# Latent pages of seven sequences turned in 32x32 blocks on VectorE instead of on TensorE

## The reference

```python
def _mla_keys(kv_lat, k_rope, w_uk, g_k_head):
    k_nope = jnp.einsum('btl,lhd->bthd', kv_lat, w_uk)
    k_r = jnp.broadcast_to(k_rope[:, :, None, :], k_nope.shape[:-1] + (QK_ROPE,)).astype(k_nope.dtype)
    return _rmsnorm(jnp.concatenate([k_nope, k_r], axis=-1), g_k_head)
...
    def absorb(carry, kv_blk, kr_blk, mask):
        m, l, acc = carry
        k = _mla_keys(kv_blk, kr_blk, w_uk, g_k_head).astype(jnp.float32)
        sc = jnp.einsum('bshd,bphd->bhsp', qf, k) * scale
...
        acc = acc * corr[..., None] + jnp.einsum('bhsp,bpl->bhsl', p, kv_blk.astype(jnp.float32))
```

## Time and profile before

| | |
|---|---|
| median of three runs | 1144.9 us (1142.89 to 1145.04) |
| the profiled execution's own time | 1145.37 us |
| its span in the profile | 1143.5 us |
| busy, share of the span | PE 98%, PEld 95%, DVE 68%, ACT 51%, POOL 6% |
| the pages of sequences 0 to 7 | about 389 to 811 us of the span |

### The profile page before, as it was taken

The page is one execution under the profiler, slowest core; times in us unless marked ns, Lnnn a source line. Parts: engine busy times, 40 slices in busy tenths (PEclk is TensorE's granted clock), DMA queues, the critical chain, the costliest instruction groups (busy, mean ns, idle before and its releaser), DMA issues.

```text
span 1143.5 us, 25908 instructions
## 1 busy us (share of the span) xinstructions
PE 1122.7 (98%) x9549; PEld 1086.8 (95%) x9549; DVE 778.4 (68%) x1325; ACT 581.7 (51%) x1153; POOL 67.8 (6%) x136
## 2 busy tenths in 40 slices
PE   5999999999999999999999999999999999999998
PEld 3899999999898899999999999999999999999998
DVE  4655553567777688888888888888757666555543
ACT  3444453346576655455545454554566545444432
POOL 2000000010000100101010110101020010000000
PEclk9999999999999999999999999999999999999999
DMA  9987578947344440021211202032257684555552
GB/s 324 314 292 269 183 254 289 348 167 222 99 142 127 133 133 2 20 65 33 52 47 36 62 22 73 13 84 71 57 150 254 227 272 131 183 183 177 177 184 71
DMA packets 165629, 169.84 MB, mean 149 GB/s; under 512 B 25780, under 2 KB 144071, under 8 KB 165525
## 3 DMA queue, kind: packets, MB, share of 16 engines
q1 hardware_dynamic: 163799, 166.83, 45.6%
q10 hardware_dynamic: 1742, 1.88, 0.5%
HBM read 167.13 MB, written 2.49 MB: 148 GB/s over the span
## 4 chain that ended last, share of the span: by engine, by line
PE 92%; DVE 2%; SPq 2%; ACT 1%; DMA 1%; issue 1%; POOL 0%; DVEq 0%; ACTq 0%
PE PS L1894 27%; PE PS L1895 27%; PE PS L1896 27%; PE PS L1971 2%; SPq L451 2%; PE PS L2367 1%; PE PS L2342 1%; PE PS L2343 1%; DMA raw<-in_w_ffn_in 1%; PE PS L2288 1%; PE PS L2099 1%; PE PS L2308 0%; PE PS L2338 0%; DVE wL L1172 0%; PE PS L2287 0%
## 5 line engine op out<-in xcount | busy, mean ns | idle before, releaser
L1172 DVE TENSOR_TENSOR wL<-raw,wH 128x1024 fp32r<-128x1024 f32 (+2 forms) x208 | 246.3, 1191 | 209.8 <-ACT wH L717 208.4
L717 ACT ACTIVATE wH<-raw 128x1024 fp32r<-128x1024 f32 (+2 forms) x208 | 213.2, 1029 | 245.6 <-PE PS L1896 224.7
L1894 PE MATMUL PS<-uH,wH 128*128 128x264 f32 x1024 | 294.2, 287 | 4.5 <-DVE uL L1233 4.0
L1895 PE MATMUL PS<-uL,wH 128*128 128x264 f32 x1024 | 291.8, 285 | 0.0
L1896 PE MATMUL PS<-uH,wL 128*128 128x264 f32 x1024 | 291.4, 285 | 0.0
L1894 PE MATMUL PS<-wqH,kTH 128*128 128x336 f32 (+2 forms) x768 | 255.7, 333 | 0.0
L1896 PE MATMUL PS<-wqH,kTL 128*128 128x336 f32 (+2 forms) x768 | 246.1, 320 | 0.0
L1895 PE MATMUL PS<-wqL,kTH 128*128 128x336 f32 (+2 forms) x768 | 245.9, 320 | 0.0
L1894 PEld LDWEIGHTS PS<-uH,wH 128*128 128x128 f32 x1024 | 193.9, 189 | 7.9 <-issue 6.4
L1895 PEld LDWEIGHTS PS<-uL,wH 128*128 128x128 f32 x1024 | 194.2, 190 | 0.0
L1896 PEld LDWEIGHTS PS<-uH,wL 128*128 128x128 f32 x1024 | 193.6, 189 | 0.0
(11 more groups left out here) (343 smaller groups left out, 1497.8 us busy)
## 6 DMA issues: line engine op xcount, KB each, us to landing
raw<-in_w_ffn_in SPq DMA_DIRECT2D x86, 512.0 KB, 3.5
adaw<-in_w_ada SPq DMA_DIRECT2D x72, 512.0 KB, 6.5
raw<-in_w_ffn_out SPq DMA_DIRECT2D x32, 512.0 KB, 3.5
raw<-in_w_in SPq DMA_DIRECT2D x32, 512.0 KB, 4.5
kv<-in_cache_kv_latent SPq DMA_DIRECT2D x128, 128.0 KB, 2.0
raw<-in_w_ffn_out SPq DMA_DIRECT2D x16, 384.0 KB, 3.0
raw<-in_w_attn_out SPq DMA_DIRECT2D x8, 512.0 KB, 4.1
raw<-in_w_conv_out SPq DMA_DIRECT2D x8, 512.0 KB, 4.7
```

Source lines behind the costliest of these rows:

```text
L717: f(wH[:, k, 0:width], raw[:, k, 0:width], ACT.Copy).then_inc(w_hi, 1)
L1172: v.tensor_tensor(wL[:, k, 0:width], raw[:, k, 0:width], wH[:, k, 0:width].bitcast(F32), ALU.subtract).then_inc(w_lo, 1)
L1894: mm(dst, a[0], b[0], start=start, stop=False)
L1895: mm(dst, a[0], b[1], start=False, stop=False)
```

## The change

For sequences 1 to 7 TensorE no longer turns the latent pages. SP copies a group of four pages inside SBUF from `kv2` into `kx`, in four transfers; transfer q takes columns 32q to 32q+31 of each half of each page and puts them into partitions 32q to 32q+31, in runs of 32 elements. VectorE transposes `kx` (128x1024) in blocks of 32x32 into `kT32`, once for a group, in steps 2, 6, 10 and 14, ahead of kTL, for the group that begins two pages later. Each has two buffers; together they take the place of `raw`, which is free between the gate weights of sequence 0 and the end of the pages. In `kT32` the tokens of a page stand in four parts; `kTH` is written through a permuted view (neighbours 4 elements apart), and kTL reads and writes in that view too, so the keys' product reads the same layout as before. kTH waits for the counter `kx_ps` instead of `kT_ps`, and for `kr_ps` where it reads rotary keys. Sequence 0 stays with TensorE.

`VALUES_PAGE` goes from 10 to 8 and the taps are given out anew. SP's loop over the sequences is written out, with the copies between the loads; `gate_quad(1)` is asked for after the last kTL.

```diff
-VALUES_PAGE = 10
-TAPS = (0, 1, 1, 0, 2, 2, 1, 2, 2, 2, 7, 3, 2, 3, 1, 2)
+VALUES_PAGE = 8
+TAPS = (0, 0, 0, 0, 2, 2, 1, 2, 5, 2, 2, 4, 3, 4, 2, 2)
...
+        kx = sb("kx", [P, 2, 4 * KL], at=ring)
+        kT32 = sb("kT32", [P, 2, 4 * KL], at=ring + 8192)
...
+        def turned_page(n):
+            return kT32[:, n // 4 % 2, :].rearrange("p (k a h t) -> p a h k t", k=4, a=4, h=2)[:, n % 4, :, :, :]
...
+            def pages_next(b, g):
+
+                sp.wait_ge(pg_rel, 4 * b + g + 1)
+                page_group(b, b % 2, g)
+
+            def blocks(b, g):
+
+                grp = 4 * (b - 1) + g
+                sp.wait_ge(kv2_in[4 * (b % 2) + g], 128 * (b // 2) + 128)
+                if grp >= 2:
+                    sp.wait_ge(kx_ps, grp - 1)
+                pages = kv2[:, NPG * (b % 2) + 4 * g:NPG * (b % 2) + 4 * g + 4, :].rearrange(
+                    "p a (h q i) -> p (a h) q i", q=4, i=QUAD)
+                for q in range(4):
+                    sp.dma_start(kx[QUAD * q:QUAD * q + QUAD, grp % 2, :], pages[:, :, q, :]).then_inc(kx_in[grp % 2], 16)
+
+            def sequence_loads(b):
+
+                if b >= 1:
+                    blocks(b, 2)
+                    blocks(b, 3)
+                if 1 <= b < NB - 1:
+                    pages_next(b + 1, 0)
+                if b < NB - 1:
+                    blocks(b + 1, 0)
+                if 1 <= b < NB - 1:
+                    pages_next(b + 1, 1)
+                    pages_next(b + 1, 2)
+                if b < NB - 1:
+                    blocks(b + 1, 1)
+                if 1 <= b < NB - 1:
+                    pages_next(b + 1, 3)
...
-            with sp.Fori(1, 4) as i:
-                sample_pages(i, 0)
-                sample_pages(i, 1)
+            sp.wait_ge(w_lo, 4 * Q_GATE + 4)
+            for b in range(NB):
+                sequence_loads(b)
+            sp.wait_ge(kTL_done, PAGES + 2)
             with sp.Fori(1, 4) as i:
                 gate_quad(i)
...
+            def page_hi(b, n, turned=False):
+                pg = NPG * b + n
+                if turned:
+                    act.wait_ge(kT_ps, n + 1)
+                else:
+                    act.wait_ge(kx_ps, 4 * b + n // 4 - 3)
                 act.wait_ge(kn_ps, pg + 1)
                 if n % 4 == 0:
+                    act.wait_ge(kr_ps, 8 * b + n // 2 + 1)
                     f(krT[:, (n // 4) % 2, :], PS[:, 0, KL:KL + P], ACT.Copy)
-                f(kTH[:, n % 2, :], PS[:, 0, 0:KL], ACT.Copy).then_inc(kTH_done, 1)
+                if turned:
+                    f(kTH[:, n % 2, :], PS[:, 0, 0:KL], ACT.Copy).then_inc(kTH_done, 1)
+                else:
+                    f(kTH[:, n % 2, :].rearrange("p (h t k) -> p h k t", h=2, k=4), turned_page(n), ACT.Copy
+                      ).then_inc(kTH_done, 1)
...
+            def turn_group(b, g):
+
+                dve.wait_ge(kx_in[g % 2], 128 * b + 64 * (g // 2) - 64)
+                dve.wait_ge(kTL_done, NPG * b + 4 * g - 2)
+                v.transpose(kT32[:, g % 2, :], kx[:, g % 2, :]).then_inc(kx_ps, 1)
+
+            def page_lo(pg, n, b, s, first, turned=False):
 
 
                 dve.wait_ge(kTH_done, pg + 1)
                 if n % 4 == 1:
+                    dve.wait_ge(kr_ps, 8 * b + n // 2 + 2)
                     own.wait()
                     own.done(v.tensor_copy(Srope[:, s, n - 1:n + 3, :],
                                            PS[:, 0, 384:448].rearrange("p (j h) -> p j h", h=H)))
                 if n == 10 and not first:
                     denominators(b - 1)
-                v.tensor_tensor(kTL[:, n % 2, :], PS[:, 0, 0:KL], kTH[:, n % 2, :].bitcast(F32), ALU.subtract
-                                ).then_inc(kTL_done, 1)
+                lo_, hi_ = kTL[:, n % 2, :], kTH[:, n % 2, :].bitcast(F32)
+                if turned:
+                    v.tensor_tensor(lo_, PS[:, 0, 0:KL], hi_, ALU.subtract).then_inc(kTL_done, 1)
+                else:
+                    v.tensor_tensor(lo_.rearrange("p (h t k) -> p h k t", h=2, k=4), turned_page(n),
+                                    hi_.rearrange("p (h t k) -> p h k t", h=2, k=4), ALU.subtract
+                                    ).then_inc(kTL_done, 1)
...
+                    if n % 4 == 2:
+                        if n + 2 < NPG:
+                            if not first:
+                                turn_group(b, (n + 2) // 4)
+                        elif not last:
+                            turn_group(b + 1, 0)
                     if not (last and n == NPG - 1):
-                        page_lo(pg + 1, (n + 1) % NPG, b, s, first)
+                        page_lo(pg + 1, (n + 1) % NPG, b, s, first, first and n + 1 < NPG)
...
-            def turn(use, s, n, pg, b, first):
+            def turn(use, s, n, pg, b, first, turned=False):
...
-                tr(PS[:, 0, 0:128], kv2[:, NPG * s + n, 0:128], ident)
-                tr(PS[:, 0, 128:256], kv2[:, NPG * s + n, 128:256], ident).then_inc(kT_ps, 1)
+                if turned:
+                    tr(PS[:, 0, 0:128], kv2[:, NPG * s + n, 0:128], ident)
+                    tr(PS[:, 0, 128:256], kv2[:, NPG * s + n, 128:256], ident).then_inc(kT_ps, 1)
```

More of the change, by code:

```diff
@@ L169, in decoder_layer @@
         vecT = sb("vecT", [P, V_N])
+        gains = base[0]
         gbc = sb("gbc", [P, B_N])
@@ L356, in decoder_layer @@
         kv2_in = [sem(f"kv2_in{g}") for g in range(8)]
+        kx_ps, kr_ps = sem("kx_ps"), sem("kr_ps")
+        kx_in = [sem(f"kx_in{g}") for g in range(2)]
         qx_done, den_ps, mx_done, gmx_done, sub_done, p_done, lsum_done = map(
@@ L1054, in sequence @@
                     pg = NPG * b + n
-                    if not (last and n == NPG - 1):
-                        page_hi(pg + 1, (n + 1) % NPG)
+                    if n + 1 < NPG:
+                        page_hi(b, n + 1, first)
+                    elif not last:
+                        page_hi(b + 1, 0)
                     if n == 1 and not first:
@@ L1066, in _ @@
             act.wait_ge(memz, 6)
-            page_hi(0, 0)
+            page_hi(0, 0, True)
             state_columns(1)
@@ L1637, in _ @@
             put_q(0, 0)
-            page_lo(0, 0, 0, 0, True)
+            page_lo(0, 0, 0, 0, True, True)
             heads_out(3)
@@ L2335, in turn @@
                 if n % 4 == 0:
-                    tr(PS[:, 0, KL:KL + P], kr2[:, s, n:n + 4, :].rearrange("p a b -> p (a b)"), ident)
+                    tr(PS[:, 0, KL:KL + P], kr2[:, s, n:n + 4, :].rearrange("p a b -> p (a b)"), ident).then_inc(kr_ps, 1)
                 if n % 4 == 1:
                     mm(PS[:, 0, 384:448], krT[:, (n // 4) % 2, :],
-                       qbd[:, ds(b, 1), :, :].rearrange("p o j h -> p (o j h)"), start=True, stop=True)
+                       qbd[:, ds(b, 1), :, :].rearrange("p o j h -> p (o j h)"), start=True, stop=True).then_inc(kr_ps, 1)
                 if n == 10 and not first:
                     denominator(b - 1, 1 - s)
-                tr(PS[:, 0, 0:128], kv2[:, NPG * s + n, 0:128], ident)
-                tr(PS[:, 0, 128:256], kv2[:, NPG * s + n, 128:256], ident).then_inc(kT_ps, 1)
+                if turned:
+                    tr(PS[:, 0, 0:128], kv2[:, NPG * s + n, 0:128], ident)
+                    tr(PS[:, 0, 128:256], kv2[:, NPG * s + n, 128:256], ident).then_inc(kT_ps, 1)
             def keys(b, sq, n, pg):
@@ L2375, in sequence @@
                     if n + 1 < NPG:
-                        turn(use, s, n + 1, pg + 1, b, first)
+                        turn(use, s, n + 1, pg + 1, b, first, first)
                     elif not last:
@@ L2403, in _ @@
                     pe.wait_ge(masked, H)
-                    turn(0, 0, 0, 0, 0, True)
+                    turn(0, 0, 0, 0, 0, True, True)
             values(H - 1)
```

8 lines of the change are left out of this document (2 added, 6 removed).

## The result

The changed kernel takes 1177.9 us (median of 4 runs, 1177.5 to 1182.0), the kernel before 1144.7 beside it: ratio 1.0301, 95% interval 1.0276 to 1.0326. It is 33.2 us slower, where I had forecast 9.4, and outside my range.

What follows compares the result with a forecast made beforehand. TensorE was taken to bound the pages, with VectorE near enough to take its place. Seven sequences at +1.3 us, -1.2 once for the last and +1.5 at the start gave +9.4 us, 1154.5 us; 8-in-10 range 1135 to 1168.

Steps and rivals of the forecast that it cites:

- The bound and the mechanism: Cached pages: TensorE sets the pace; after the change long VectorE steps make kTL late and TensorE waits for it.
- The lengths: VectorE and ScalarE in the pages: wide transpose 1.24 us, kTL +0.18 us, kTH about +0.24 us.
- The upper end for the 16-byte step: Permuted kTH and kTL: the stride costs as much as the trace's widest strides, +0.18 and about +0.24 us, not nothing.
- rival 1: Permuted kTH and kTL: the stride costs nothing, so -6 us, 1139 us; chance 0.27.
- The waits: Page stage: TensorE idles 4.8 us a sequence for kTL, most at page 15, some at pages 3 and 7.
- The sum of 9.4: Whole kernel: 7 x 1.3 - 1.2 + 1.5 = +9.4 us.
- the start: Sequence 0: first pieces land at 439 to 440.5, then transposing; +1.5 us, between 0.5 and 5.
- VectorE's steps: Pages: instruction lengths added per step and compared with TensorE's 2.84 us page; steps 10 to 14 make 14.9 us.
- TensorE's saving: Sequences 1 to 7: two transposes fewer a page, 0.22 us, 3.5 us a sequence, 24.6 us in all.
- Rival 2: Page stage: TensorE keeps nearly all of the 24.6 us saved, 1122 us; chance 0.07.
- Rival 3: Transfers inside SBUF: pieces come late, 4 us once a sequence adding 28 us, 1180 us; chance 0.10.
- the margin: Pieces of a sequence's first two groups: they land 1.5 to 3 us before VectorE wants them, so cost nothing.

Runs made afterwards that it cites:

- e1: Changed kernel with plain views of kTH and kTL, no 16-byte step (result differs): 1158.6 us, 19 us less than the change.
- e8: Changed kernel with the 16-byte step moved from kTH and kTL into VectorE's transposing instruction, same result: 1179.3 us.
- e4: Changed kernel with the loops over pairs of sequences of TensorE, VectorE and ScalarE written out: 1164.7 us.
- e14: e11 with VectorE's transposing instruction moved from ahead of the subtraction to kTL to behind the reduction of its step: 1130.0 us.
- e7: Kernel before the change with its three loops over pairs of sequences written out, nothing else: 1143.5 us.
- e5: Kernel before the change without 29 of the 31 taps of every sequence (result differs): 1143.7 us.
- e3: Changed kernel with the transposing of sequence 1's first group moved from head to end of step 14 of sequence 0: 1176.8 us.
- e12: Kernel before, loops written out, plus all 448 transfers of pieces inside SBUF, read by nobody: 1144.1 us.
- e11: Changed kernel without 29 of the 31 taps and with plain views of kTH and kTL: 1150.5 us.
- e13: e11 with SyncE issuing the pieces of the next sequence's second group ahead of its pages 8 to 11: 1149.2 us.
- e6: Changed kernel without 29 of the 31 taps of every sequence: 1153.2 us.
- e2: Changed kernel without most of GpSimd's work of sequences 0 to 7, its waits and signals kept: 1177.1 us.
- e15: Change for only the last eight pages of each sequence, loops written out, transposing behind the reduction of its step: 1139.6 us.
- e17: e15 with the transposing right behind the subtraction to kTL, ahead of tap and reduction: 1139.7 us.
- e18: e4 with the transposing right behind the subtraction to kTL instead of ahead of it: 1166.3 us.

## Why the prediction was wrong

**The bound and the mechanism: right.** VectorE took TensorE's place, TensorE waits for kTL and for nothing else that is new, and the likeliest case was "slower". (The forecast's own numbers add up to 1154.3, not 1154.5.)

**The lengths: right.** Transposing 1.23 us (1.24 from rows 5, 7 and 8), kTL +0.19 (0.18), kTH +0.26 (0.24). The upper end for the 16-byte step was the right one: e1 gives 19 us back, so rival 1 is refuted. Of the Trainium skill's two pages, the measurement bears out the section SBUF Cachelines of Advanced Engine Details and Errata, and not Door 1 of SBUF — State Buffer, by which four fp32 would still be free: kTL took 0.615 us against 0.415, and the transposing 2.0 against 1.23 (e8).

**The waits: right in size and place.** I had TensorE waiting 4.8 us a sequence. The rows of its waits for kTL give 35.5 / 7 = 5.1 us in the changed kernel and 26.8 / 7 = 3.8 written out (e4). Between sequences it is more: in e4 a mean one takes 379.8 / 7 = 54.3 us, the one of e14 shown above 49.6, 4.7 us less. Three of the four waits of e4's sequence 5 stand at the rotary transpose behind a transposing of VectorE (0.7, 0.8, 1.6 us), the longest of them at page 15, where I had it.

**What failed, with its size.** The sum of 9.4 was 1.5 for the start and 7.9 for the seven sequences; the marks give 6.1 and 26.2.
1. *The loops, 11.5 us, the largest.* They had no term in my sum. I read rows 5 to 7 for the lengths of VectorE's steps and did not ask what it pays at the two jumps back and for waits on registers, because TensorE covered it before (0.7 us in all). e4 and e7 put it at 12.2 and 0.7 us, with 1.7 us in the 12.2 for the sequence at half clock. It is the step "VectorE's steps": I costed the work and not the issue around it. How much of it is the jumps and how much the waits on registers, the runs don't tell.
2. *TensorE's saving, less its waits: 6.7 us.* Written out, 54.3 against 52.2 us is +2.1 a sequence, 14.6 in all where I had 7.9. Since the waits came out near my 4.8, it is the saving that was too large: rows 3 give 0.11 us a transpose, and 2.85 us for a light page came true, but I multiplied by all 16 pages. e5 and e14 show 2.5 us a sequence instead of 3.5, and TensorE's busy time falls by 1.8 only (52.2 to 50.4 in e4). A page that is late for another reason, as page 3 of e14, keeps nothing of what it saves.
3. *The start, 4.6 us.* The four issues took 2.9 us (434.33 to 437.26), not 2, and the pieces landed 4.6 us behind them, not 1.7: VectorE waited till 441.86, I had 439 to 440.5, and then 1.2 us of turning stand ahead of kTL. TensorE waited for 4.2 us, and the page behind, at granted clock 0.50, took 5.3 us from start to start, where the same page takes 3.1 in e14's sequences. These 2.2 us had no term in my sum. The 6.1 us lie over my upper bound of 5. In e3 moving this one instruction gets back about 1 us of the time; in e14, with all of them moved, the first mark lies 1.0 us behind that of e5.
The three make 22.8 us; 9.4 + 22.8 = 32.2, against 32.0 of span. They are differences between the same marks, so that they add up is no proof of their causes.

**Rival 2 (TensorE gets nearly all)** fails, but for a reason I had only half: two buffers of kTH, and an instruction ahead of kTL that nobody needs yet. **Rival 3 (late pieces)**: after the start VectorE waits for no pieces in the changed kernel. The price was low, though. Over the seven sequences the DMA share is 0.52 of 392.0 us, before 0.17 of 365.9; the difference, 142 us x 16 over the 114688 runs of 28 groups, is some 20 ns a run, against my 11 to 13. e12 against e7 (0.58 and 0.17 of 365.2 us) gives 21. Pieces were late in e11 and e13, when VectorE ran faster: the margin was as thin as stated, and the slow VectorE hid it.

**Range.** Its upper end came from "late pieces" alone. A term that is zero only because another engine covers it belonged in it.

**Left open.** Which of the 29 taps hold the 24.7 us of e6 was not tested; the one beside `krq`, ahead of a kTL, is a suspect that e2 left in place. The 3.65 us page of e15 and e17 isn't explained. No run separates the half clock from the wait ahead of it. In the pages of the profiled executions of e1, e3, e4, e14, e18 and the change every such stretch stands at a wait of TensorE of 1.9 to 4.2 us, and the change's wait of 2.2 us has none.

## What to carry to other kernels

When a change hands the bound to another engine, list what that engine pays besides its instructions: jumps back, waits on registers, hand-overs. A measurement in the kernel before doesn't show it: written out, its pages gained 0.7 us, those of the changed kernel 12. And never put a long instruction ahead of the short one that another engine waits for: with room on VectorE its place alone was 20 us. Look at the granted clock behind each new wait of TensorE, which here made the wait at the start half as long again. Moving half of a load beat moving all of it: with loops written out on all sides, e15 is 3.9 us below e7, e4 21 above.

## What the runs showed of the hardware

- A step of 16 bytes costs VectorE 0.75 to 0.78 ns an fp32 element, in a subtraction (0.20 us for 256, e1 against the change) and in a transposing instruction (0.76 us for 1024, e8) alike, and ScalarE's copy 0.25 us for 256.
- The 32x32 transposing of 128x1024 fp32 in SBUF takes 1.23 us.
- A transfer inside SBUF of 128 KB in runs of 128 bytes lands in 4.5 us (median), one of 128 KB from the cache in 2.0, and the former held the DMA engines for some 20 ns a run.
- VectorE stood still for 2.5 and 3.0 us at the jumps back of its loop, 1.5 to 1.7 where it had less to do.
- At waits of TensorE of 4.2 and 2.8 us its granted clock fell to 0.50 (1.2 GHz) for 6.8 and 3.4 us, the first within the wait, the second 0.6 us behind it. At a wait of 2.2 us it stayed at 1.00 in the change and fell for 3.4 us in e3.
- A tap of VectorE that takes 0.48 us alone took 1.05 to 1.22 us beside GpSimd's product `krq` (604.57 in the change, 603.26 in e2).
